# A bidirectional recurrence with its state made first, and its late half solved on 64 columns

## What is computed

```python
def step(state, inp):
    r_t, w_t, k_t, v_t, a_t, b_t = inp
    sa = jnp.einsum('bhvk,bhk->bhv', state, a_t)
    state = state * w_t[:, :, None, :] + sa[..., None] * b_t[:, :, None, :] + v_t[..., None] * k_t[:, :, None, :]
    return state, jnp.einsum('bhvk,bhk->bhv', state, r_t)
```

## Time and profile before

| | |
|---|---|
| runs, median (lowest to highest) | 1768.61 us (1767.59 to 1771.94), 3 runs |
| profiled execution | 1770.21 us, of it span 1768.4 us |
| PE busy | 1700.8 us, 96% |
| DVE, ACT, POOL busy | 48%, 19%, 12% |
| DMA | 460.43 MB, mean 260 GB/s |
| the recurrence's four turns | 652.87 to about 884 us |
| expert stage | 944 to 1768 us |

### The profile page before, as it was taken

The page is one execution under the profiler, slowest core; times in us unless marked ns, Lnnn a source line. Parts: engine busy times, 40 slices in busy tenths (PEclk is TensorE's granted clock), DMA queues, the critical chain, the costliest instruction groups (busy, mean ns, idle before and its releaser), DMA issues.

```text
span 1768.4 us, 31384 instructions
## 1 busy us (share of the span) xinstructions
PE 1700.8 (96%) x13280; PEld 1121.5 (63%) x13280; DVE 844.0 (48%) x1949; ACT 341.7 (19%) x726; POOL 220.3 (12%) x301
## 2 busy tenths in 40 slices
PE   8999999999999999989879999999999999999997
PEld 6888886688545568878736555555555555555553
DVE  6666653655658456676325333443334333333331
ACT  3334333122011334533201000000001000010101
POOL 2431430000001423741200000000000000000000
PEclk9999999999999999999988999999999999999999
DMA  9542517544641110100656999999999999999995
GB/s 324 190 171 74 184 52 234 190 150 184 192 161 56 32 23 12 34 20 8 247 226 252 384 377 428 426 428 424 427 426 427 426 427 427 426 426 426 428 426 239
DMA packets 111119, 460.43 MB, mean 260 GB/s; under 512 B 28016, under 2 KB 56960, under 8 KB 89472
## 3 DMA queue, kind: packets, MB, share of 16 engines
q1 hardware_dynamic: 108928, 457.07, 65.2%
q10 hardware_dynamic: 2048, 1.31, 0.2%
HBM read 456.26 MB, written 2.10 MB: 259 GB/s over the span
## 4 chain that ended last, share of the span: by engine, by line
PE 86%; DVE 6%; DMA 5%; ACT 2%; issue 1%; SPq 0%; POOL 0%; DVEq 0%; ACTq 0%; POOLq 0%
PE ps L1593 19%; PE ps L813 15%; PE ps L995 12%; PE ps L867 10%; PE ps L1568 9%; PE ps L1603 6%; DMA arena<-mw 4%; PE ps L1575 3%; PE ps L1163 2%; PE ps L859 1%; PE ps L1510 1%; PE ps L821 1%; PE ps L1524 1%; PE ps L1009 1%; PE ps L887 1%
## 5 line engine op out<-in xcount | busy, mean ns | idle before, releaser
L1593 PE MATMUL ps<-arena 128*64 128x256 f32 x3584 | 397.8, 380 | 6.2 <-DMA arena<-mw 6.2
L1593 PEld LDWEIGHTS ps<-arena 128*64 128x64 f32 x3584 | 256.7, 137 | 160.4 <-issue 30.2
L813 PE MATMUL ps<-arena 128*128 128x128 f32 (+10 forms) x2226 | 336.7, 322 | 20.4 <-DVE arena L2558 9.2
L813 PEld LDWEIGHTS ps<-arena 128*128 128x128 f32 (+2 forms) x2226 | 253.9, 186 | 90.4 <-issue 56.0
L2899 DVE TENSOR_TENSOR arena<-arena,ps 64x256 f32<-64x256 f32 x140 | 59.5, 425 | 459.0 <-ACT arena L2086 458.9
L995 PE MATMUL ps<-arena 128*128 128x256 f32 x952 | 210.7, 379 | 0.1
L1568 PE MATMUL ps<-arena 128*64 128x512 f32 x896 | 203.2, 597 | 4.0 <-DMA arena<-mw 2.2
L995 PEld LDWEIGHTS ps<-arena 128*128 128x128 f32 x952 | 178.5, 190 | 23.8 <-issue 0.5
L867 PE MATMUL ps<-arena 128*128 128x256 f32 (+1 forms) x714 | 189.0, 425 | 0.0
L2086 ACT ACTIVATE arena<-ps 64x256 f32<-64x256 f32 x140 | 52.8, 377 | 680.9 <-PE ps L1593 590.4
L867 PEld LDWEIGHTS ps<-arena 128*128 128x128 f32 x714 | 134.8, 190 | 50.6 <-issue 34.4
(11 more groups left out here) (290 smaller groups left out, 1394.5 us busy)
## 6 DMA issues: line engine op xcount, KB each, us to landing
arena<-mw SPq DMA_DIRECT2D x168, 2048.0 KB, 26.7
arena<-wqkv SPq DMA_DIRECT2D x35, 1024.0 KB, 7.4
arena<-fw SPq DMA_DIRECT2D x32, 1024.0 KB, 7.4
arena<-wrkv SPq DMA_DIRECT2D x12, 1024.0 KB, 7.4
arena<-awo SPq DMA_DIRECT2D x4, 1024.0 KB, 6.3
arena<-bwo SPq DMA_DIRECT2D x4, 1024.0 KB, 9.0
arena<-rows SPq DMA_DIRECT2D x4, 384.0 KB, 4.8
arena<-xp SPq DMA_DIRECT2D x2, 512.0 KB, 4.6
```

Source lines behind the costliest of these rows:

```text
L813: last = mm(o, a, b, start=(n == 0), stop=(n == len(pairs) - 1))
L1593: last = mm(ps[r, g % 4, 0:256], picked[:, b, k, 0:64], w[:, k, a * 256:(a + 1) * 256], start=(k == 0), stop=(k == KB - 1))
```

## The change

The state is made first. `state()`, the same 32 matmuls that stood in the late chain, is now issued right behind `early_y` (in the loaded turns that is between `system(nq, 1)` and `operands(nq, 2)`), in bank 5 + 16 % 3, and DVE makes S0 from it before `off_blocks`. In the late chain, between E of direction 0 and ET of direction 1, two new groups `keys_by_state` multiply the late half's keys with S0; DVE adds them to z0l, the right-hand side. The late chain z1 to z5 then runs on 64 columns. The output of the state, queries times S0, is added to y by `state_y`, one half behind z3 and one behind z4. Gone are `late_keys` and its semaphore, the products `Rq` and DVE's additions for `Rp`. DVE's `off_blocks` and `inverse_rows` are divided anew. Apart from this, behind the last turn ScalarE's wait for head_done and its router DMA move from ahead of the copies to moT to between the second and the third.

The diff without its unchanged lines:

```diff
--- before.py
+++ after.py
@@ -340,9 +340,8 @@
-        Rp = [m.take(2, P) for _ in range(2)]
-        z0l = [m.take(4, P) for _ in range(2)]
+        z0l = [m.take(4, RH) for _ in range(2)]
@@ -369,7 +368,7 @@
-        zl = [[lent.take(4, P) for _ in range(2)] for _ in range(2)]
+        zl = [[lent.take(4, RH) for _ in range(2)] for _ in range(2)]
@@ -439,9 +438,9 @@
-        St, Rq, Y = Pair("St"), Pair("Rq"), Pair("Y")
+        St, KS, Y = Pair("St"), Pair("KS"), Pair("Y")
-        mo_ok, al_sb = sem("mo_ok"), sem("al_sb")
+        mo_ok = sem("mo_ok")
@@ -747,7 +746,6 @@
-            sp.wait_ge(al_sb, 2 * NQ)
@@ -1304,7 +1302,7 @@
-                turn = [16 * late]
+                turn = [17 * late]
@@ -1381,51 +1379,70 @@
+                def state():
+                    bank = 5 + 16 % 3
+                    for d in range(2):
+                        pe.wait_ge(ke_ok[d], 2 * (q + 1))
+                        k = keb[q % 2][d]
+                        for h in range(4):
+                            r, c = slice(h % 2 * RH, h % 2 * RH + RH), slice(h * RH, (h + 1) * RH)
+                            at = (2 * d + h // 2) * RH
+                            last = run(ps[r, bank, at:at + RH], [(k[:, 0, c], value(q, d, h)), (k[:, 1, c], ze[d][0][:, h, :])])
+                    last.then_inc(St.ps, 1)
+                def keys_by_state(n, d):
+                    for h in range(4):
+                        last = by_halves(ps[:, 5 + n % 3, h * RH:(h + 1) * RH], [(ar_late[q % 2][d][:, h // 2, 0, :], S0[d][:, h, :])])
+                    last.then_inc(KS.ps, 1)
+                def state_y(d):
+                    for h in range(4):
+                        add_y(1 - d, h, ar_late[q % 2][d][:, h // 2, 1, :], S0[d][:, h, :])
+                    state()
+                    state()
+                pe.wait_ge(St.sb, 4 * (q + 1))
+                keys_by_state(19, 0)
+                need(ET, 1, 0)
+                keys_by_state(20, 1)
+                turn[0] += 2
+                need(E, 1, 0)
-                need(ET, 1, 0)
+                pe.wait_ge(KS.sb, 2 * q + 1)
-                need(E, 1, 0)
-                pe.wait_ge(al_sb, 2 * (q + 1))
-                four(z1, gt_of(0, 1), z0l[0])
+                pe.wait_ge(KS.sb, 2 * q + 2)
+                four(z1, gt_of(0, 1), z0l[0], RH)
-                four(z1, gt_of(1, 1), z0l[1])
+                four(z1, gt_of(1, 1), z0l[1], RH)
-                bank = 5 + turn[0] % 3
-                turn[0] += 1
-                for d in range(2):
-                    pe.wait_ge(ke_ok[d], 2 * (q + 1))
-                    k = keb[q % 2][d]
-                    for h in range(4):
-                        r, c = slice(h % 2 * RH, h % 2 * RH + RH), slice(h * RH, (h + 1) * RH)
-                        at = (2 * d + h // 2) * RH
-                        last = run(ps[r, bank, at:at + RH], [(k[:, 0, c], value(q, d, h)), (k[:, 1, c], ze[d][0][:, h, :])])
-                last.then_inc(St.ps, 1)
+                four(E2T, Em[0], ETm[0])
-                four(E2T, Em[0], ETm[0])
+                four(E2T, Em[1], ETm[1])
-                four(E2T, Em[1], ETm[1])
-                pe.wait_ge(St.sb, 4 * (q + 1))
-                four(z2, ETm[0], zl[0][0])
+                four(z2, ETm[0], zl[0][0], RH)
-                four(z2, ETm[1], zl[1][0])
+                four(z2, ETm[1], zl[1][0], RH)
@@ -1435,28 +1452,20 @@
-                    four(z3, E2Tm[d], zl[d][1])
+                    four(z3, E2Tm[d], zl[d][1], RH)
+                state_y(0)
-                    four(z4, E2Tm[d], zl[d][0])
+                    four(z4, E2Tm[d], zl[d][0], RH)
+                state_y(1)
-                    four(z5, E2Tm[d], zl[d][1], P, late_rows[d])
-                bank = 5 + turn[0] % 3
+                    four(z5, E2Tm[d], zl[d][1], RH, late_rows[d])
-                        r, at = slice(h % 2 * RH, h % 2 * RH + RH), d * S + h // 2 * P
-                        last = run(ps[r, bank, at:at + P], [(zl[d][0][:, h, RH:P], gm1[2 * d + 1][:, h, :])])
-                last.then_inc(Rq.ps, 1)
-                for d in range(2):
-                    for h in range(4):
-                        add_y(1 - d, h, gm1[2 * d + 1][:, h, :], zl[d][0][:, h, 0:RH])
-                pe.wait_ge(Rq.sb, 2 * (q + 1))
-                for d in range(2):
-                    for h in range(4):
-                        last = add_y(1 - d, h, Rp[d][:, h // 2, :], S0[d][:, h, :], last=True)
+                        last = add_y(1 - d, h, gm1[2 * d + 1][:, h, :], zl[d][0][:, h, :], last=True)
@@ -1961,14 +1970,7 @@
-                act.activation(z0l[d][:, :, 0:RH] if i % 2 else z0e[d], src, ACT.Copy).then_inc(z0.sb, 1)
-            def late_keys(q, d):
-                if q:
-                    act.wait_ge(z1.ps, chain(q - 1, 1, d))
-                act.wait_ge(ops_ok[d], 4 * (q + 1))
-                act.activation(z0l[d][:, :, RH:P], dirs[d]["E"][:, 1 - d, 1, :].rearrange("p (h n) -> p h n", h=4), ACT.Copy).then_inc(al_sb, 1)
+                act.activation(z0l[d] if i % 2 else z0e[d], src, ACT.Copy).then_inc(z0.sb, 1)
@@ -2010,24 +2012,22 @@
-                at[0] = 16
+                at[0] = 17
+                out_of(ET, 1, 0, ETm[0])
+                out_of(E, 1, 0, Em[0])
+                at[0] = 21
+                out_of(ET, 1, 1, ETm[1])
+                out_of(E, 1, 1, Em[1])
-                    out_of(ET, 1, d, ETm[d])
-                    out_of(E, 1, d, Em[d])
-                for d in range(2):
-                    out_of(z1, 1, d, zl[d][0])
-                at[0] = 23
+                    out_of(z1, 1, d, zl[d][0], RH)
-                if nq:
-                    late_keys(nq, 0)
-                    late_keys(nq, 1)
-                act.activation(gate.rearrange("p t n -> p (t n)"), ps[:, 5 + 27 % 3, :], ACT.Copy).then_inc(gate_sb, 1)
-                at[0] = 30
+                act.activation(gate.rearrange("p t n -> p (t n)"), ps[:, 5 + 29 % 3, :], ACT.Copy).then_inc(gate_sb, 1)
+                at[0] = 32
-                    out_of(z4, 1, d, zl[d][1])
+                    out_of(z4, 1, d, zl[d][1], RH)
@@ -2052,15 +2052,14 @@
-            late_keys(0, 0)
-            late_keys(0, 1)
-            act.wait_ge(head_done, NQ + 1)
-            act.dma_start(rw, router.rearrange("(k p) n -> p k n", p=P)).then_inc(in_router, 16)
+                if b == 2:
+                    act.wait_ge(head_done, NQ + 1)
+                    act.dma_start(rw, router.rearrange("(k p) n -> p k n", p=P)).then_inc(in_router, 16)
@@ -2586,16 +2585,15 @@
-                    width = P if late else RH
-                    dve.tensor_tensor(dst.rearrange("p a b -> p (a b)"), bank(n)[:, 0:4 * width], src.rearrange("p a b -> p (a b)"), ALU.add).then_inc(s.sb, 1)
+                    dve.tensor_tensor(dst.rearrange("p a b -> p (a b)"), bank(n)[:, 0:RQ], src.rearrange("p a b -> p (a b)"), ALU.add).then_inc(s.sb, 1)
-                    width, r = P if late else RH, (slice(RH, P), slice(0, RH))[d]
+                    r = (slice(RH, P), slice(0, RH))[d]
-                    dve.tensor_tensor(a, ps[r, 5 + n % 3, 0:4 * width], a, ALU.add).then_inc(z5.sb, 1)
+                    dve.tensor_tensor(a, ps[r, 5 + n % 3, 0:RQ], a, ALU.add).then_inc(z5.sb, 1)
@@ -2624,39 +2622,40 @@
-                    off_blocks(nq, 0)
-                    off_blocks(nq, 1)
-                    off_blocks(nq, 2)
-                    off_blocks(nq, 3)
-                        dve.tensor_tensor(S0[d][r, f::2, :], ps[r, 5 + 22 % 3, 2 * d * RH:2 * (d + 1) * RH].rearrange("p (a n) -> p a n", a=2),
+                        dve.tensor_tensor(S0[d][r, f::2, :], ps[r, 5 + 16 % 3, 2 * d * RH:2 * (d + 1) * RH].rearrange("p (a n) -> p a n", a=2),
-                chain_step(z2, 25, 1)
+                if nq:
+                    off_blocks(nq, 0)
+                    off_blocks(nq, 1)
+                dve.wait_ge(z0.sb, 4 * (q + 1))
+                for d in range(2):
+                    z = z0l[d].rearrange("p a b -> p (a b)")
+                    dve.wait_ge(KS.ps, 2 * q + d + 1)
+                    dve.tensor_tensor(z, bank(19 + d)[:, 0:RQ], z, ALU.add).then_inc(KS.sb, 1)
+                if nq:
+                    off_blocks(nq, 2)
+                    off_blocks(nq, 3)
+                chain_step(z2, 27, 1)
-                chain_step(z3, 28, 1)
+                chain_step(z3, 30, 1)
-                chain_step(z5, 32, 1)
+                chain_step(z5, 34, 1)
-                    inverse_rows(nq, 8, 11)
-                dve.wait_ge(Rq.ps, q + 1)
-                for d in range(2):
-                    dve.tensor_tensor(Rp[d], ps[:, 5 + 34 % 3, d * S:(d + 1) * S].rearrange("p (a n) -> p a n", a=2),
-                                      ar_late[q % 2][d][:, :, 1, :], ALU.add).then_inc(Rq.sb, 1)
-                if nq:
-                    inverse_rows(nq, 11, 14)
+                    inverse_rows(nq, 8, 13)
-                    inverse_rows(nq, 14, BLK)
```

(1 more changed line is left out.)

## The result

The changed kernel takes 1749.4 us (median of four runs, 1747.8 to 1750.3) against 1768.1: a ratio of 0.988, interval 0.987 to 0.990. Forecast were 1746 and a range of 1739 to 1757. The profiled execution took 1750.27 us, span 1748.4, so 20.0 us of span less, where the sum said 22.75.

A forecast was written before the change was run, and what follows sets the result against it. DVE bounds a loaded turn's last 20 us, TensorE the rest and the fourth turn, then a pause of 8.90 us follows. Gains 7.35 + 3.6 + 11.8 = 22.75 us gave 1747.5 profiled, 1746 median, range 1739 to 1757.

The forecast's parts named there:

- Steps 1 to 3: Loaded turn up to z2: moved state 0, keys_by_state +1.2 us, late z1 1.78 to 1.04; z2 begins 0.5 us later.
- Step 4: TensorE's late chain from z2 to the end of y in a loaded turn: 12.99 us become 7.75.
- Step 5: DVE's ledger in loaded turns: inverse ends 2.45 us earlier, capping TensorE's own 4.7; three turns gain 7.35 us.
- rival b: Loaded turns: longer pauses cost TensorE its clock in all three, + 2.7 us, so 1748.7; 15%.
- Step 6: Fourth turn, z2 to end of y: 11.96 us become 7.75, less 0.5 for later z2; gain 3.6.
- Step 7: Behind the last turn, transposes to L1524: 28.49 us become 16.7, gain 11.8; the router's DMA stays hidden.
- Step 8: Expert stage: shifts as a whole with its weight stream and passes the tail's gain on, at no cost.
- Rival a): Late chain: narrow products are no shorter than wide ones, 0.89 us each, so 1753; 3%.
- c): Loaded turns gain nothing: late blocks, DVE's wait for the state and the moved row eat it, so 1753; 6%.
- e): Loaded turns give TensorE's whole 4.7 us, so 1739; 6%.
- d): Expert stage: weights set the end, so the tail's gain of 11.8 us is lost, 1757; 8%.
- f): Slower: half-clock spells of 6.8 us in each loaded turn and the tail, 27.3 in all, so 1773; 3%.

The follow-up runs named there:

- experiment 6: Changed kernel with the state's 32 matmuls moved behind the systems instead of ahead of operands 2; 1749.0 us in one run.
- experiment 3: Changed kernel with the late chain's z1 to z4 done with whole 128-column weights instead of split halves; 1761.2 us in one run.
- tail_alone: Kernel before with only ScalarE's wait for head_done and router DMA moved between the second and third copy to moT; 1758.05 us, ratio 0.993.
- recurrence_alone: Changed kernel with the move of ScalarE's head_done wait and router DMA undone; 1761.9 us, ratio 0.9955.
- after_again: The changed kernel itself, run again as the base for later versions on the same chip; 1750.7 us, ratio 0.9885.
- experiments 2 and 5: 2: both kernels without inverse rows 8 to 15 in loaded turns, 4.0 us apart per turn; 5: changed kernel, y's copy on ScalarE, 1745.35 us, with fillers 1746.5.
- state_behind: Changed kernel with state() moved behind system(nq, 3); 1749.0 us in one run.
- experiment 1: The change's two parts singly: the head_done and router DMA move on the kernel before, 1758.05 us; the changed kernel without that move, 1761.9 us.
- experiment 4: Changed kernel with useless matmuls in TensorE's pauses in the loaded and fourth turns; 1747.0 us, ratio 0.986.
- fillers2: Changed kernel with useless 128x256 matmuls behind the loaded turns' first pairings, ahead of the fourth, and ahead of the wait for GT; 1747.0 us, ratio 0.986.

## Why the prediction was right, and where it was short

**Steps 1 to 3** held. z2 began 0.75 later in its turn, forecast 0.5. The late blocks cost nothing (experiment 6), and neither did DVE's wait for the state, behind which it is still idle for 4.11 us.

**Step 4** held: 7.57 us measured, 7.75 forecast. That narrow products are short held too, and experiment 3 shows that they are so only with split weights.

**Step 5**, the ledger of DVE, is the best part. The copy of y came 3.3 us earlier in its turn (forecast 3.2), the end of the inverse 2.7 (2.45), and the two waits of TensorE were 2.25 and 2.76 (2.2 and 3.0). Three turns gave 7.5 (7.35), though the clock fell in each. That the sum agrees to 0.2 us is luck: the trace of before has a fall of its own in the second turn (1.5 us by rival b), and other traces of the same two recurrences have 195.1 us for the three turns before (tail_alone, where before has 196.8) and 190.3 and 190.4 after (recurrence_alone, after_again; 189.3 in the first). From pair to pair the gain is 4.7 to 7.5. The mechanism is shown by experiments 2 and 5. TensorE's own gain, which the ledger capped, was put at 4.7 and is 4.67.

**Step 6**, the fourth turn, was mis-sized: 2.55 us instead of 3.6. The arithmetic of its chain was on the safe side (7.32 instead of 7.75), but the first products behind the wait for GT met the clock at 0.63 and took 5.35 us for 32 records, where before they took 3.84:

```profile
843.74 5.35 PE L811 MATMUL ps<-arena 128*128 128x128 f32 x32 [2.08 <-DMA arena<-td]
```

In state_behind, whose fourth turn has the same instructions, the clock held there: 3.84 us for the 32, and 30.25 for the turn, 4.06 less than before. So the chain's gain was there, and what the step put at nothing was the clock behind the wait for GT.

**Step 7** held to 0.2 us. The full clock for all 32 products was part of it, and is in the trace. The router's DMA went out at 884.4, 8.9 us behind the transposes, took 14.4 us (13.1 before) and was there well before its first reader at 907.12.

**Step 8** held as far as the gain went through. Its expert stage differs by 1.4 us from before, but the stage took 823.5 to 825.4 us in the traces of all these kernels, none of which changes it; so I call that scatter, not a cost.

**The chances.** The loss in the table's first line lies in the first products of the program, 15.97 us for L1007's 32 records instead of 14.00, which the change doesn't touch (14.0 to 17.1 us in the traces of this document); with the fourth turn's 1.05 it makes up nearly all of the 2.8 us between the forecast and the profiled execution. The median is 3.4 above the forecast, as the profiled execution lies 0.9 above it and not 1.6.

Rival b), the clock, did happen as told, in all three turns, and its 1748.7 is nearer to the median than my 1746. The nearness is luck: b) charged 2.7 us to the loaded turns (two more spells at its 1.5 would be 3.0), and they have no loss against the sum; the loss came in the fourth turn and at the program's start, which b) doesn't name. Still I had given it 15% because one turn in three showed it; with pauses that I had myself worked out to grow from 0.86 to 2.2 and from 2.2 to 3.0 us the falls should have been the likeliest case.

Rival a) falls by the 7.57 us of the late chain, c), e) and g) by the table, and d) by experiment 1 and the waits for weights. Of f)'s four spells of 6.8 us none came: without those in the turns the first two are 0.7 and 1.3 us shorter (experiment 4), and over the 32 products of the tail the clock was 1.00.

## What to carry to other kernels

When a solve is made shorter on one engine, write the ledger of the engine that will be late next before counting the gain: here 4.7 us of TensorE's became 2.5 per loaded turn. Look for waits that stand ahead of work they don't guard: one such wait, moved by two copies, gave more than the whole rewriting of the recurrence. And count each pause that grows as a risk for TensorE's clock.

## What the runs showed of the hardware

The same program met the falls of the clock at different places in two executions: in after_again two windows more are low than in the first trace, 0.57 in each of them.

```profile
712.00:716.00 4.00, 4.00 (x69) 0.57 0.27 31
...
828.00:832.00 4.00, 4.00 (x50) 0.57 0.01 2
```

The recurrence took 223.2 us there and 221.0 in the first trace. 1.0 us of the difference lies in the fourth turn's first 32 products, 6.38 us instead of 5.35. Matmuls that fill a pause from its beginning kept the clock at 1.00 in every turn of fillers2; matmuls put in after it had fallen, behind the router, ran at half with the rest (0.51 in 905 to 919).
